# One block for the preparation and the scan of a state-space layer, with its filler work spread anew

## The reference, cut to what matters

```
pl = h @ w_in                                  # z | x,B,C | dt | v, gate
xs, B, C = split(silu(dwconv5(x,B,C)))         # 16 heads of 64; 4 groups of 128 states
dt = softplus(dt_raw + dt_bias)                # per token, direction and head
la = dt * (-exp(a_log)); acum = cumsum(la, in chunks of 128 tokens)
for each direction d in (forward, backward), each chunk in that order, each head:
    y += ((C B^T) * exp(acum_l - acum_s), masked) @ (xs*dt)   # inside the chunk
    y += exp(acum) * C @ state                                # from earlier chunks
    state = exp(acum_end) * state + (B * exp(acum_end - acum))^T @ (xs*dt)
o_ssd = rmsnorm((y + d_skip * xs) * silu(z))
o_cf  = silu(layernorm(dwconv31(v * sigmoid(gate))))    # "depthwise taps"
out   = [o_ssd, o_cf] @ w_out
```

## Time and profile before

| | us |
|---|---|
| median of 3 runs | 2557.86 (2557.3 to 2558.94) |
| the profiled execution, its own time | 2558.41 |
| its span in the trace | 2556.6 |
| TensorE busy | 2193.2 (86%) |
| VectorE busy | 1681.2 (66%) |
| ScalarE busy | 1333.6 (52%) |
| GpSimd busy | 281.0 (11%) |

### The profile page before, as it was taken

How to read it: one execution, slowest core, us unless ns; L and a number is a source line. 1 busy time by engine, 2 the same in 40 slices (tenths; PEclk the granted TensorE clock), 3 DMA queues, 4 the chain that set the end, 5 groups by cost and what they waited for, 6 DMA issues and landing times. The chain is left out here.

```text
span 2556.6 us, 36052 instructions
## 1 busy us (share of the span) xinstructions
PE 2193.2 (86%) x12176; PEld 1796.2 (70%) x12176; DVE 1681.2 (66%) x2815; ACT 1333.6 (52%) x2092; POOL 281.0 (11%) x355
## 2 busy tenths in 40 slices
PE   5999799989987999948887699995889986699994
PEld 4899676679974666737666687884678774577773
DVE  5884235368624479986663599995567754599994
ACT  2663214356423255656443388883476641488882
POOL 0000000000000056556100001101000000011100
PEclk8999899999988999969999699997898987699997
DMA  5554331456532766500021499996221111499992
GB/s 213 169 184 151 125 102 50 140 182 198 173 103 75 257 236 234 220 17 1 17 73 51 157 368 386 389 394 244 78 80 58 58 59 66 162 388 394 396 389 79
DMA packets 127254, 454.95 MB, mean 178 GB/s; under 512 B 13824, under 2 KB 17792, under 8 KB 126976
## 3 DMA queue, kind: packets, MB, share of 16 engines
q1 hardware_dynamic: 116160, 413.14, 44.5%
q0 software_dynamic: 10944, 39.85, 4.1%
HBM read 431.97 MB, written 20.97 MB: 177 GB/s over the span
## 5 line engine op out<-in xcount | busy, mean ns | idle before, releaser
L2525 DVE TENSOR_TENSOR moe_w_lo<-ring,moe_w_hi 128x1024 fp32r<-128x1024 f32 x384 | 462.7, 1222 | 62.4 <-ACT moe_w_hi L2463 57.4
L2463 ACT CAST moe_w_hi<-ring 128x1024 fp32r<-128x1024 f32 x384 | 399.0, 1049 | 147.6 <-PE ps L236 120.4
L373 DVE TENSOR_TENSOR ffn_w_lo<-ring,ffn_w_hi 128x1024 fp32r<-128x1024 f32 x132 | 161.0, 1223 | 101.6 <-ACT ffn_w_hi L325 101.4
L234 PE MATMUL ps<-moe_w_hi,moe_own 128*128 128x512 f32 x512 | 214.3, 419 | 12.1 <-DVE moe_own L2532 11.1
L235 PE MATMUL ps<-moe_w_lo,moe_own 128*128 128x512 f32 x512 | 205.1, 401 | 0.0
L236 PE MATMUL ps<-moe_w_hi,moe_own 128*128 128x512 f32 x512 | 205.0, 400 | 0.0
L325 ACT CAST ffn_w_hi<-ring 128x1024 fp32r<-128x1024 f32 x132 | 137.4, 1044 | 107.8 <-PE ps L236 107.8
L234 PE MATMUL ps<-ffn_h_hi,ffn_w_hi 128*128 128x256 f32 x608 | 173.3, 285 | 11.1 <-DVE ffn_w_lo L373 11.1
L235 PE MATMUL ps<-ffn_h_lo,ffn_w_hi 128*128 128x256 f32 x608 | 172.0, 283 | 0.0
L236 PE MATMUL ps<-ffn_h_hi,ffn_w_lo 128*128 128x256 f32 x608 | 172.0, 283 | 0.0
L2375 POOL DMA_INDIRECT moe_got<-token_rows,moe_idx x32 | 44.6, 1393 | 903.8 <-DVE moe_idx L2520 903.8
(11 more groups left out here) (487 smaller groups left out, 5487.9 us busy)
## 6 DMA issues: line engine op xcount, KB each, us to landing
ring<-in_weights SPq DMA_DIRECT2D x766, 512.0 KB, 5.3
expert_rows<-moe_y POOLq DMA_DIRECT2D x32, 512.0 KB, 7.3
token_rows<-moe_token_rows SPq DMA_DIRECT2D x6, 512.0 KB, 2.7
sq<-in_cmp_w SPq DMA_DIRECT2D x1, 2048.0 KB, 7.7
both<-in_x SPq DMA_DIRECT2D x1, 1024.0 KB, 5.8
both<-in_context SPq DMA_DIRECT2D x1, 1024.0 KB, 8.1
out<-both SPq DMA_DIRECT2D x1, 1024.0 KB, 4.8
cols<-in_cols SPq DMA_DIRECT2D x1, 720.5 KB, 9.2
```

What stands on the lines that cost most here:

```text
L234: pe.matmul(out, w_hi, x_hi, start=start, stop=False)
L373: dve.tensor_tensor(w_lo[:, u % WB], k.ring[:, (first + u) % RING], w_hi[:, u % WB], ALU.subtract).then_inc(w_split, 1)
L2463: act.copy(w_hi[:, j % WB].rearrange("p h f -> p (h f)"), k.slot(act, first + GU + j, e).rearrange("p a f -> p (a f)")).then_inc(w_rounded, 1)
L2525: dve.tensor_tensor(w_lo[:, j % WB].rearrange("p h f -> p (h f)"), k.ring[:, (first + GU + j) % RING].rearrange("p a f -> p (a f)"), w_hi[ ...
```

## The change

1. `ssd_prep` and `ssd_scan` become one block, `ssd`, without a barrier between them. Each engine's list is the preparation's followed by the scan's, cut shorter as below, and new semaphores (`rows_made`, `decayed`, `sums`) stand for what the barrier gave.
2. Token groups: the first 6 of 12 are turned and copied before the scan; group 6+u is copied by ScalarE in unit u; TensorE turns 6 and 7 after `front(1)`, and 8 to 11 behind `front` in the loop, in banks 2 and 3.
3. The decay sums are three products (two with 64 columns, one with 128) in place of 16; they stand behind the 8 products for `ac_t`.
4. Tile 6's taps: the middle one and six more go into `even_in`'s list (`LATE_FROM` 7), whose loop over m takes two entries after the second split instead of one; the other 24 taps, 48 half taps, go 4, 5 and 2 in the preparation, then two behind `back(u-1)` for u of 1 to 8, one for u of 9 to 28, and one at the end.
5. `EARLY` is 4: tile 7's taps 0 to 3 in the preparation, one in each of units 0 to 26.
6. The product of y by `ssd_d` on ScalarE goes; VectorE folds it into the first addition to each part of y (s of 0 and 2), as two instructions of 128 columns in place of one of 256.
7. Before `spread` of every group VectorE waits until its token groups are copied; TensorE waits in front of `front(0)` for `rows_made` and six copies, and in `front(8)` for all.

```diff
-POOLED, PAIRED, ALONE, LATE_ALONE, LATE_POOLED = (2, 4, 5), (0, 1), (3,), 6, 7
+POOLED, PAIRED, ALONE, LATE_ALONE, LATE_POOLED, LATE_FROM = (2, 4, 5), (0, 1), (3,), 6, 7, 7
...
-                work = [(tiles, j) for tiles in (PAIRED, ALONE) for j in cf_order()]
+                work = [(tiles, j) for tiles in (PAIRED, ALONE) for j in cf_order()] + [((LATE_ALONE,), j) for j in cf_order()[:LATE_FROM]]
...
                     second_split(2 * m)
-                    take_taps(filled)
+                    take_taps(2 * filled)
...
-    EARLY = 16
+    EARLY = 4
...
+        GROUPS, FIRST = TT * 3, TT // 2 * 3
+        def group_bank(n):
+            return n % 5 if n < FIRST else 2 + n % 2
...  (TensorE, after the definitions of front and back)
+                for n in range(4):
+                    turn_tokens(n)
+                pe.wait_ge(la_ready, 1)
+                for c in range(TT):
+                    for d in range(2):
+                        mm = pe.matmul(k.ps[d * ROWS_D:d * ROWS_D + SH, 5, c * P:(c + 1) * P], la[:, c, d, :], tri[:, d, :],
+                                       start=True, stop=True)
+                mm.then_inc(across, 1)
+                for d in range(2):
+                    pe.matmul(k.ps[:, 6, 0:TT * 2 * SH].rearrange("p (t d h) -> p t d h", t=TT, d=2)[:, :, d, :], tri[:, d, :], la[:, :, d, :],
+                              start=True, stop=True)
+                pe.matmul(k.ps[:, 7, 0:TT * 2 * SH], k.ones[:, :], la_flat, start=True, stop=True).then_inc(sums, 1)
+                for n in range(4, FIRST):
+                    turn_tokens(n)
+                pe.wait_ge(cleared, 1)
+                pe.wait_ge(rows_made, 1)
+                pe.wait_ge(kept, FIRST)
                 front(0)
                 front(1)
+                pe.wait_ge(ended, 1)
+                turn_tokens(FIRST)
+                turn_tokens(FIRST + 1)
                 for u in range(NU):
                     back(u)
                     if u + 2 < NU:
                         front(u + 2)
+                    if FIRST + 2 + u < GROUPS:
+                        turn_tokens(FIRST + 2 + u)
...  (GpSimd)
+                for i in range(EARLY):
+                    take_tap(i)
+                pool.wait_ge(decayed, 1)
+                weigh(0)
+                for u in range(NU):
+                    if u % SG == 0 and u // SG + 1 < NU // SG:
+                        weigh(u // SG + 1)
+                    take_tap(EARLY + u)
+                    if 2 * SG <= u < NU - 2 * SG:
+                        fade(u)
...  (ScalarE)
+                for n in range(4):
+                    keep_tokens(n)
+                    late_tap(n)
+                act.wait_ge(across, 1)
+                act.wait_ge(cleared, 1)
+                for d in range(2):
+                    own = slice(d * ROWS_D, d * ROWS_D + SH)
+                    act.copy(ac_t[own, :, :].rearrange("p c l -> p (c l)"), k.ps[own, 5, :]).then_inc(rounded, 1)
+                for n in range(4, FIRST):
+                    keep_tokens(n)
+                act.wait_ge(ended, 1)
+                act.activation(to_end[:, :, :, :], to_end[:, :, :, :], ACT.Exp)
+                act.activation(cdec[:, :, :, :], cdec[:, :, :, :], ACT.Exp).then_inc(decayed, 1)
...  (ScalarE, in each unit behind its exponentials)
-                    if EARLY + u < CFK:
-                        scale_tap(act, EARLY + u, late_added, u).then_inc(late_scaled, 1)
+                    if FIRST + u < GROUPS:
+                        keep_tokens(FIRST + u)
+                    late_tap(EARLY + u)
...  (VectorE)
-                    ad = dve.tensor_tensor(yy, yy, k.ps[:, 6 + u % 2, 0:GW].rearrange("p (a l) -> p a l", a=2), ALU.add)
+                    if s % 2 == 0:
+                        for i in range(2):
+                            m = 2 * g + i
+                            ad = dve.scalar_tensor_tensor(y[:, m, tok], y[:, m, tok], skip[:, m:m + 1],
+                                                          k.ps[:, 6 + u % 2, i * P:(i + 1) * P], ALU.mult, ALU.add)
+                    else:
+                        yy = y[:, 2 * g:2 * g + 2, tok]
+                        ad = dve.tensor_tensor(yy, yy, k.ps[:, 6 + u % 2, 0:GW].rearrange("p (a l) -> p a l", a=2), ALU.add)
...
+                dve.scalar_tensor_tensor(la_flat, dt_flat, -1.0, dt_flat, ALU.mult, ALU.max).then_inc(dt_abs, 1)
+                late_taps(4)
...  (aneg, dt, la, pick_head, never as before)
+                late_taps(5)
...  (the low parts of ac_t, then rows_made; wait for sums; acum, cdec, nacum, to_end, then ended)
+                dve.wait_ge(kept, 3)
                 spread(0)
+                late_taps(2)
                 for u in range(NU):
                     if u % SG == 0 and u // SG + 1 < NU // SG:
+                        dve.wait_ge(kept, GROUPS if u // SG + 1 >= TT else FIRST)
                         spread(u // SG + 1)
                     front(u)
                     if u:
                         back(u - 1)
                         if u - 1 >= NU - SG:
                             dve.drain()
                             gate(u - 1)
+                        else:
+                            late_taps(2 if u <= 2 * SG else 1)
                 back(NU - 1)
                 dve.drain()
                 gate(NU - 1)
+                late_taps(len(pieces))
```

More of the change, by code:

```diff
@@ L1689, in ssd @@
         la_flat = la[:, :, :, :].rearrange("p t d h -> p (t d h)")
[L1690 to L1805, removed]
-                for d in range(2):
-                    own = slice(d * ROWS_D, d * ROWS_D + SH)
-                    low = slice(2 * ROWS_D + d * ROWS_D, 2 * ROWS_D + d * ROWS_D + SH)
-                    dve.tensor_tensor(ac_t[low, :, :].rearrange("p c l -> p (c l)"), k.ps[own, 5, :],
-                                      ac_t[own, :, :].rearrange("p c l -> p (c l)"), ALU.subtract)
-                late_taps(len(alone))
@@ L1834, in front @@
                               never[:, d, :].unsqueeze(1).broadcast_to([P, SREP, P]), start=True, stop=False, skip_group_check=True)
+                    if u == 2 * SG:
+                        pe.wait_ge(kept, GROUPS)
                     for h in range(SREP):
@@ L1921, in _, with late_taps @@
             @block.vector
             def _(dve):
+                pieces = [(j, part) for j in cf_order()[LATE_FROM:] for part in range(2)]
+                def late_taps(count):
+                    for j, part in pieces[:count]:
+                        o, i = list(tap_parts(late_u[:, 0, :], cf[:, LATE_ALONE], j))[part]
+                        dve.scalar_tensor_tensor(o, i, ftaps[:, LATE_ALONE, j:j + 1], o, ALU.mult, ALU.add)
+                        if part:
+                            dve.drain()
+                    del pieces[:count]
@@ new lines, in _ @@
+                dve.tensor_scalar(never[:, :, :], tri[:, :, :], 1.0, -NEG, ALU.subtract, ALU.mult)
+                late_taps(5)
+                for d in range(2):
+                    dve.wait_ge(rounded, d + 1)
+                    own = slice(d * ROWS_D, d * ROWS_D + SH)
+                    low = slice(2 * ROWS_D + d * ROWS_D, 2 * ROWS_D + d * ROWS_D + SH)
+                    lw = dve.tensor_tensor(ac_t[low, :, :].rearrange("p c l -> p (c l)"), k.ps[own, 5, :],
+                                           ac_t[own, :, :].rearrange("p c l -> p (c l)"), ALU.subtract)
@@ new lines, in _ @@
+                lw.then_inc(rows_made, 1)
+                dve.wait_ge(sums, 1)
+                flat = [a[:, :, :, :].rearrange("p t d h -> p (t d h)") for a in (acum, to_end, nacum, cdec)]
+                dve.tensor_copy(flat[0], k.ps[:, 6, 0:TT * 2 * SH])
+                dve.tensor_copy(flat[3], k.ps[:, 7, 0:TT * 2 * SH])
+                dve.drain()
+                dve.tensor_scalar(flat[2], flat[0], -1.0, None, ALU.mult)
+                dve.tensor_tensor(flat[1], flat[3], flat[0], ALU.subtract).then_inc(ended, 1)
```

90 lines of the change are left out of this document (68 added, 22 removed).

## The result

The changed kernel takes 2543.42 us (median of 4 runs, 2542.92 to 2543.97) against 2557.67 for the kernel before in the same comparison: ratio 0.9944, 95% interval 0.9928 to 0.9959, 14.3 us less. I had forecast 2530, 27.6 us less, with a range of 2522 to 2543; the measured time lies 0.4 us above it. The direction was right; about half of the gain is missing. The profiled execution has a span of 2541.2 us, 15.4 less than before.

What follows compares the result with a forecast made beforehand. The preparation was taken as bound by filler half taps on VectorE, the scan by TensorE plus waits around `spread`. The terms -34.5 + 2.0 + 2.5 + 2.0 + 0.4 = -27.6 us gave 2530, range 2522 to 2543.

Steps and rivals of the forecast that it cites:

- start of the scan: Preparation up to the scan's first `back`: that product comes 34.5 us earlier, bounds 31.5 to 35.5.
- `even_in`: Block taking in seven taps of tile 6: +2.0 us, from 1.2 at its end and 0.8 for crowding.
- units 0 to 7: First eight scan units, with turned groups and two half taps each: +2.5 us, bounds -1 and +7.
- units 8 to 31: Later scan units: half taps fit VectorE's room; +2.0 us, 0.5 in each of four groups, bounds 0 and 15.
- the end: Behind the last gate: one half tap, +0.41 us, summed as 0.4.
- my own signs of being wrong: First `back` later than 20 us, scan groups above 16 us, or TensorE gaps between `even_in` steps 9 and 18.
- The clock stays at its lower level: Scan: rival with TensorE at 1.2 GHz throughout, 60 us more, 2590, slower than before; chance 0.02.
- The scan stretches: Scan: rival with half taps ahead of the product TensorE waits for in every unit; 12 us, 2540; chance 0.19.
- `even_in` stalls: `even_in`: rival with six added entries delaying splits, TensorE dry between steps 9 and 18; 14 us, 2543; chance 0.08.
- the crowding: `even_in` around steps 13 to 17, where VectorE's spare room is about one entry: +0.8 us, bounds -0.5 and 14.
- the entry in step 36: `even_in`, steps 24 to 39: one more entry, VectorE finishing last, paid in full at 0.8 to 1.56 us, 1.2 taken.
- that rule for the half taps: Scan: VectorE and GpSimd exclude each other; fully blocked, an unlucky half tap takes 1.1 us and no longer fits, 2544.

Runs made afterwards that it cites:

- e9: Changed kernel with VectorE's wait for token copies only in units 0 and 11, not ahead of `spread` in units 4 to 20: 2534.07 us, ratio 0.9897.
- e5: Changed kernel with one more GpSimd wait, so the fade of units 11, 15, 19, 23 starts after VectorE's `spread`: 2535.4 us, ratio 0.9925.
- e1: Changed kernel with three filler products on TensorE in units 8, 12, ... 28, in the gap behind `spread`: 2533.23 us, ratio 0.9911.
- e6: Changed kernel with the 20 single half taps of tile 6 moved from units 9 to 28 to behind the last gate: 2552.07 us, ratio 0.9986.
- e4: Changed kernel with tile 6's first seven taps moved out of `even_in` to behind the last gate: 2544.37 us, ratio 0.9942.
- e10: Kernel before with one needless wait, for exponentials made long before, ahead of `spread` in units 4 to 24: 2560.38 us, ratio 1.0009.
- e2: Changed kernel with `spread` and `weigh` of each next group one unit later (4k+1 instead of 4k): 2532.27 us, ratio 0.9895.
- e3: Kernel before with three small VectorE copies behind each `spread` from unit 8 on: 2577.86 us, ratio 1.0069.
- e7: Kernel before with only the decay sums changed, three products in place of 16: 2554.12 us, ratio 0.9992.

## Why the prediction was wrong, step by step

| step | forecast, us | measured, us |
|---|---|---|
| start of the scan, block start to first `back` | -34.5 | 16.4 instead of 49.8: -33.4 |
| `even_in` | +2.0 | its first product to the next block's first VectorE instruction 288.8, then 291.5: +2.7 |
| units 0 to 7 | +2.5 | 22.5, then 24.0: +1.5 |
| units 8 to 31 | +2.0 | 80.8, then 93.7: +12.9 |
| the end, last gate to the next block's first product | +0.4 | 0.8, then 1.25: +0.5 |
| what stands ahead and behind, unchanged | 0 | -1.8 and +2.1 |
| sum | -27.6 | -15.4 of span (the rounded parts give -15.5) |

**The step that failed** is "Units 8 to 31 ... Taken +2.0": it has no term for the granted clock, which it took to stay at 1.00. The sum of the terms that it has was right: with the clock held by the old order of `spread` and `fade` (e9) the stage takes 83.0 us, +2.2. Its make-up was luck: I had put 0.5 on each of four groups, and in e9 units 8 to 11 take 15.4 us instead of 13.9, the next three groups only 0.2 more each, the rest 0.1. What is missing is 93.7 - 83.0 = 10.7 us, of which the needless waits ahead of `spread` are the cause (e9, e5) and the granted clock the carrier (e1: 93.7 - 84.4 = 9.3 with the long `spread` left in). I had the wait in the list of the change, and named what GpSimd's new wait holds up, but not what VectorE's holds up: I took a wait that is met as free. And I read the gap of 1.7 us as a loss of TensorE's time only, 11.8 us over 15, not as something on which the clock hung. Of my own signs of being wrong, two came: groups above 16 us, and a gap of TensorE in step 14 of `even_in`.

**The rivals.** "The clock stays at its lower level" had the right mechanism, in part: 23.9 us of the scan at 1.2 GHz rather than all of it. I gave it 0.02 because TensorE was 86% busy, and a mean over the stage says nothing of how its longest gap stands. "The scan stretches" came out near it in time (2540) for the wrong reason: without the 20 half taps the stage is only 0.4 us shorter (e6). "`even_in` stalls" did happen in small: step 14 takes 1.8 us longer, 1.46 of it one gap of TensorE, and steps 13 and 17 to 18 some 0.9; e4 gives the whole as 2.8 us, inside the bounds. That my +2.0 came near is luck too: the crowding cost 2.5 where I had 0.8, and the entry in step 36, paid in full by my count with 1.2, left the end of the block only 0.2 later.

**The start of the scan** went nearly as laid out: the block starts 0.95 later than before, so my 1113.3 for `ac_t`'s low parts becomes 1114.25 (measured 1114.44) and my 1113.6 for `front(0)` 1114.55 (1114.88). The two half taps beside GpSimd's `weigh` took 2.50 us where I had left 0.8, and that is where the missing 1.1 us went. The Trainium skill ("SBUF — State Buffer", Who interferes with whom) has the two engines exclude each other where VectorE's instruction has two SBUF inputs and GpSimd's reads SBUF. The trace agrees, and more closely than I allowed: the fade takes 0.61 when it goes first (changed kernel) and 1.65 when `spread` does (e9), and `spread` then takes 1.67 and 1.23. I had weighed that rule for the half taps, and the pair that mattered was `spread` and `fade`.

**Open.** Why gaps of 1.79 us bring the clock down once a group in the changed kernel and in e6, in three groups of e4, and only once in e10. The record of the clock has only its two levels, and no run here varied the place of the gap alone. That the changed scan keeps falling once it has fallen is seen (the group grows to 17.25 us and the next gap comes 17.25 later), not explained. Nor is it shown why single executions of e1 and e5 took as long as the changed kernel; their lower mean clock speaks for the same fall, but they have no trace.

## What to carry to other kernels

Read the longest recurring gap of TensorE as a risk to its clock and not only as lost time, and prefer to take a long VectorE instruction out of it (e2, stage 80.4 us) over filling it (e1, 84.4). A wait that is already met is not free on an engine that races another for the same release: put it where the engine has nothing to win, once, and not ahead of each use. When a stage slows with the same instructions in it, look at the granted clock before the work lists.

## What the runs showed of the hardware

- A second wait on a VectorE instruction, met long before, moved its start from 0.04 to 0.11 us behind the releasing product (e9 against the changed kernel; e10 against the kernel before the same).
- Of two instructions on VectorE and GpSimd released by the same product, the one that starts second has the longer time in the trace (0.61 or 1.65 us for the fade, 1.23 or 1.67 for `spread`); which is first was decided by 0.03 us.
- Three copies of 128x32 on VectorE beside GpSimd's `xw` took 2.47 us together (e3).
- Three more products of 256 columns in TensorE's gap made the kernel some 10 us faster in three of four executions (e1).
- The granted clock fell at 12 of 16 gaps of 1.79 us, at none of 12 of 1.70, and once behind one of 1.58 (changed kernel, e4, e6, e10; kernel before, e7, e9; e4).
